# Expert weights of a hybrid decoder trunk: from the 36th matrix of a layer on, two matrices per transfer into neighbouring buffers

## The chip, the core and the metric

One Trainium2 chip, one NeuronCore of it. The metric is the device time of one execution in microseconds (us), as the median of several runs. All numbers are float32.

## What is computed

Two decoder layers on 256 tokens of 1024 features. Each layer is a mixer (one input projection, three groups of attention-like heads, one output projection) and then a mixture of 32 experts, of which each token uses 2 from one group of 8. The change touches the loading of the expert weights only. The part of the reference that reads them:

```python
D_MODEL = 1024; SEQ = 256; DEPTH = 2
N_EXPERTS = 32; TOP_K = 2; D_EXPERT = D_MODEL // 4      # 256

def hierarchical_moe(h, router_group, router_expert, router_bias, expert_gate, expert_up, expert_down):
    tok = h.reshape(b * t, d)
    ...                      # combine[n, e]: weight of expert e for token n, 2 of 32 are not zero
    for e in range(N_EXPERTS):
        y = (jax.nn.silu(tok @ expert_gate[e]) * (tok @ expert_up[e])) @ expert_down[e]
        out = out + combine[:, e:e + 1] * y.astype(jnp.float32)

for l in range(DEPTH):
    x = x + mixer(rms_norm(x, norm_mix[l]))
    x = x + hierarchical_moe(rms_norm(x, norm_ffn[l]), ...)
x = rms_norm(x, norm_final)
```

## The kernel before, in words

**Matrices and buffers.** The weights of a layer's experts are 96 MiB. On the host they are cut into 96 blocks of 1 MiB, called matrices here and numbered 0 to 95 in each layer (so the 36th is number 35). A block is 128 partitions by 2048 numbers, that is 8 KB per partition. Eight sets of four experts (QUADS) take 12 matrices each (QSLOTS): four of gate weights, four of up, four of down. Gate and up matrices hold a piece of all four experts, so every one of the first eight has to be there before the set's hidden layer is finished. SBUF has room for 25 such blocks: a ring of 12 that the mixer's weights use too, two of more_buf (N0, N1), and eleven more that the mixer gives back when it no longer needs them (C and D, S0 to S3, K and K2, L, Y, X). expert_slots (L120) lists them in the order in which they are filled, and the list is gone through again and again.

**The order of loads.** load_plan (L125) works out on the host, for each load, which buffer it fills and which use of that buffer must be over. SyncE issues nearly all transfers from one queue, in program order. For expert matrix m (L535 to L554) it waits until the buffer's last reader is counted, then issues one DMA of 1 MiB and goes on:

```python
                    b, need, _ = loads[l][NMIX + m]
                    if need:
                        sync.wait_ge(freed[need[0]], need[1])
                    src = (e_gate, e_up, e_down)[m % 12 // 4]
                    sync.dma_start(slot[b], src[l, 4 * (m // 12) + m % 4]).then_inc(arrived[b], 16)
```

The loads of the next layer's mixer weights (L515) stand behind matrix 95 in the same queue; behind the second layer's stands the final gain (L556).

**The work on them.** TensorE takes the sets in order (L1068). How many rounds a set needs depends on the routing: 32 tokens per expert fit in one, and a set of which an expert has more is gone through twice with the same weights. A round is: eight matrices of gate and up, 16 matmuls each (L1089), each preceded by a wait for the matrix (slot_of, L1072); the gather of the next round's tokens, 32 matmuls (L1058); two transposes (L1103); four down matrices, 8 matmuls each (L1110), with the sums back to the tokens between them (L1118 in the first layer, L1122 in the second), four of them between matrix 10 and matrix 11 of the set. The matmuls of L1089, L1058 and L1110 are in the program once and run in a loop; the counts here are the trace's, in which each matmul of the program stands as two. GpSimd (L587 to L589) counts a matrix as freed when TensorE is done with it in the set's last round. After the last set of layer 0 comes the second layer's mixer (L669 on), after that of layer 1 the final norm (L1424 to L1438).

Of the kernel before, what the change touches and what calls it, by code (L numbers as in the profile page):

```python
# [30 lines left out]
P = 128  # L31
LAYERS = 2
D = 1024
T = 256
# [11 lines left out]
RING = 12  # L46
WARM = 10
SLOT = 2048
# [35 lines left out]
NMIX = NPROJ + D // COLS  # L84
NMOE = 3 * EXPERTS
# [33 lines left out]

def expert_slots(ring):  # L120

    return ["N0", "N1"] + ring[0:8] + ["C", "D", "S0", "S1", "K2", "S3", "S2", "K"] + ring[8:10] + ["L"] + ring[10:12] + ["Y", "X"]


def load_plan():  # L125


    ring, last, count, landed, plan = list(range(RING)), {}, {"mix": 0, "moe": 0}, {}, []

    def gone(b, of, turns):  # L130
        count[of] += 1
        last[b] = (of, count[of])
        turns.setdefault(b, []).append(last[b])

    for _ in range(LAYERS):
        wide = expert_slots(ring)
        turns = {b: [last.get(b)] for b in ring + wide[0:2]}
        for i in range(NPROJ):
            gone(ring[i % RING], "mix", turns)
        for b in wide[10:]:  # L140
            gone(b, "mix", turns)
        mixed = count["mix"]
        for m in range(NMOE):
            gone(wide[m % len(wide)], "moe", turns)
        loads = []
        for b in [ring[i % RING] for i in range(NMIX)] + [wide[m % len(wide)] for m in range(NMOE)]:
            landed[b] = landed.get(b, 0) + 16
            loads.append((b, turns[b].pop(0), landed[b]))
        plan.append((loads, wide[NMOE % len(wide)], last["D"][1], last["Y"][1], mixed))
        ring = sorted(ring, key=lambda b: last[b][1])  # L150
    return [p[0] for p in plan], plan[-1][1], last, [p[2] for p in plan], [p[3] for p in plan], [p[4] for p in plan]

# [26 lines left out]

def trunk(nc, x_in, consts, level_masks, params, w_mix, router_w, e_gate, e_up, e_down, gain_final, row_store, out):  # L180
    loads, gain_slot, last_use, scratch_free, y_free, last_mix = load_plan()
    bank_of, uses, per_layer = {}, [0] * 8, {}
# [4 lines left out]
    with ExitStack() as ctx:  # L187
        def sb(name, shape, dt=F32):
            return ctx.enter_context(nc.sbuf_tensor(name, shape, dt))
# [41 lines left out]
        slot["K2"] = work[:, 1536 + SLOT:1536 + 2 * SLOT]  # L231
        shapes = sb("shapes", [P, NKEPT + SLOT])
        slot["C"] = shapes[:, NKEPT:NKEPT + SLOT]
        slot["D"] = sb("scratch", [P, SLOT])[:, :]
        part, o = {}, 0
# [241 lines left out]
        QSLOTS = 12  # L477
# [5 lines left out]
        def _(sync):  # L483
# [14 lines left out]
            for l in range(LAYERS):  # L498
# [3 lines left out]
                for i in range(1 - l, NMIX):  # L502
# [25 lines left out]
                    if l and i == 5:  # L528
# [5 lines left out]
                        sync.dma_start(lvl_raw, level_masks).then_inc(lvl_in, 16)  # L534
                for m in range(NMOE):  # L535
                    if m == 2:
# [7 lines left out]
                    if m == 7:  # L544
                        sync.wait_ge(mix_ready, upto(l, mix_ready, GP))
                        for h in range(MH):
                            r = 32 * (h // 2) + 4 + h % 2
                            sync.dma_start(mem[h // 2][64 * (h % 2):64 * (h % 2) + 64, :],
                                           row_store[l, 1, r:r + 1, :].to_broadcast([64, T])).then_inc(floors_in, 16)
                    b, need, _ = loads[l][NMIX + m]  # L550
                    if need:
                        sync.wait_ge(freed[need[0]], need[1])
                    src = (e_gate, e_up, e_down)[m % 12 // 4]
                    sync.dma_start(slot[b], src[l, 4 * (m // 12) + m % 4]).then_inc(arrived[b], 16)  # L554
            sync.wait_ge(moe_freed, last_use[gain_slot][1])
# [40 lines left out]
        def _(pe):  # L596
# [53 lines left out]
            for l in range(LAYERS):  # L650
# [417 lines left out]
                for q in range(QUADS):  # L1068
# [3 lines left out]
                    def slot_of(m):  # L1072

                        b, _, landed = loads[l][NMIX + QSLOTS * q + m]
                        pe.wait_ge(arrived[b], landed)
                        return slot[b]
# [919 lines left out]
```

## Time and profile before

| | us |
|---|---|
| median of 3 runs | 810.07 |
| lowest and highest | 808.99, 810.78 |
| the profiled execution, its own time | 808.36 |
| its span (first to last instruction) | 806.6 |
| TensorE busy | 770.0 (95%) |
| VectorE busy | 311.9 (39%) |
| ScalarE busy | 206.2 (26%) |

The profile is of one execution. "PE" is TensorE's matmuls, "PEld" its weight loads, which overlap them, "DVE" VectorE, "ACT" ScalarE, "SPq" the instruction stream of SyncE. A row of a timeline gives the start, the length, the engine, the line in the kernel, what was written and read, how many instructions are merged, and in brackets the idle time before them with what ended it. The granted clock (PEclk) is 1.00 at 2.4 GHz and 0.50 at 1.2 GHz. All times inside the profile count from the start of the span.

The span in words: a mixer to about 213 us, the first layer's experts to 404, a mixer to 613, the second layer's experts to 801, the final norm.

### The profile page before, as it was taken

The numbers are of one execution on the slowest core, as the hardware profiler recorded it, in microseconds if no ns is written. First come the engines' busy times: TensorE is split into PE (matmuls) and PEld (weight loads), VectorE is DVE, ScalarE is ACT, GpSimd is POOL, SyncE is SP. The second block draws the span as 40 slices with busy tenths as digits, with TensorE's granted clock in tenths as the row PEclk, the third lists the DMA queues.
The fourth block names the chain that finished last, engine by engine and source line by source line (L and its number), as shares of the span: only waits on it lengthen the run. The fifth ranks groups of instructions, "written<-read, shape, count | busy, mean of one in ns | idle before, by whom it ended". The sixth has DMA issues, their size and how long they took to land.

```text
span 806.6 us, 16492 instructions
## 1 busy us (share of the span) xinstructions
PE 770.0 (95%) x6468; PEld 548.2 (68%) x6468; DVE 311.9 (39%) x747; ACT 206.2 (26%) x436; POOL 2.9 (0%) x11
## 2 busy tenths in 40 slices
PE   8999999999999998799999999999999999999966
PEld 7877888878755554466588778888787555555523
DVE  4767343762711111111268654346635111111102
ACT  2444541531400000000124554327212000010003
POOL 0000000000000000000000000000000000000000
PEclk9999999999999999999999999999999999999998
DMA  9983264598599999999998522556977999999995
GB/s 349 418 254 101 84 234 163 158 365 358 205 423 419 419 422 418 420 422 419 420 414 287 166 105 72 222 191 237 365 304 295 422 421 420 422 419 421 420 420 227
DMA packets 44329, 256.59 MB, mean 318 GB/s; under 512 B 5024, under 2 KB 12512, under 8 KB 15456
## 3 DMA queue, kind: packets, MB, share of 16 engines
q1 hardware_dynamic: 43680, 254.77, 79.8%
q8 instruction: 49, 0.80, 0.4%
q10 hardware_dynamic: 576, 0.81, 0.3%
q14 instruction: 24, 0.20, 0.1%
HBM read 252.88 MB, written 1.64 MB: 316 GB/s over the span
## 4 chain that ended last, share of the span: by engine, by line
PE 68%; DVE 13%; DMA 13%; issue 3%; ACT 2%; SPq 1%; DVEq 0%; ACTq 0%; POOLq 0%
PE ps L1089 13%; PE ps L640 10%; PE ps L1058 8%; PE ps L1110 7%; PE ps L958 6%; PE ps L1122 4%; DMA space<-e_up 4%; DMA ring<-e_down 3%; DMA late_buf<-e_down 3%; PE ps L1118 3%; DVE xn L1474 3%; PE ps L792 3%; PE ps L849 2%; PE ps L818 2%; PE ps L669 2%
## 5 line engine op out<-in xcount | busy, mean ns | idle before, releaser
L640 PE MATMUL ps<-hT,ring 128*128 128x256 f32 x800 | 183.4, 383 | 0.1
L640 PEld LDWEIGHTS ps<-hT,ring 128*128 128x128 f32 x800 | 148.8, 190 | 22.9 <-issue 3.2
L1058 PEld LDWEIGHTS ps<-hT,xn 128*128 128x128 f32 x640 | 74.0, 194 | 9.9 <-issue 7.8
L1058 PE MATMUL ps<-hT,xn 128*128 128x128 f32 x640 | 77.8, 281 | 1.9 <-DVE hT L1821 1.9
L1089 PE MATMUL ps<-space,hT 128*32 128x256 f32 x992 | 62.9, 396 | 11.0 <-DMA space<-e_up 7.8
L958 PE MATMUL ps<-xn,ring 128*128 128x256 f32 x256 | 57.8, 382 | 0.0
L1110 PE MATMUL ps<-ring,space 128*32 128x512 f32 x416 | 51.0, 598 | 7.0 <-ACT space L1415 6.6
L1089 PEld LDWEIGHTS ps<-space,hT 128*32 128x32 f32 x992 | 30.7, 113 | 38.4 <-DMA space<-e_up 12.0
L1821 DVE TENSOR_TENSOR hT<-shapes,sel 128x128 f32<-128x128 f32 x40 | 9.9, 288 | 112.1 <-PE ps L1096 111.9
L958 PEld LDWEIGHTS ps<-xn,ring 128*128 128x128 f32 x256 | 48.2, 190 | 7.1 <-issue 0.7
L1890 DVE COPY hT<-ps 128x512 f32<-128x512 f32 x18 | 12.4, 691 | 89.1 <-PE ps L1110 89.1
L1838 DVE TENSOR_TENSOR hT<-ps,gffn 128x512 f32<-128x512 f32 x40 | 27.6, 691 | 49.7 <-PE ps L1058 49.7
L1411 ACT ACTIVATE hT<-ps 128x256 f32<-128x256 f32 x18 | 6.9, 383 | 154.4 <-PE ps L1089 154.4
L1089 PE MATMUL ps<-ring,hT 128*32 128x256 f32 x752 | 44.7, 380 | 0.0
L1415 ACT ACTIVATE space<-ps 128x256 f32<-128x256 f32 x18 | 6.9, 383 | 142.3 <-PE ps L1103 142.3
L1118 PEld LDWEIGHTS ps<-space,hT 128*128 128x128 f32 x144 | 25.2, 190 | 18.7 <-ACT hT L1417 7.5
L1118 PE MATMUL ps<-space,hT 128*128 128x256 f32 x144 | 36.1, 394 | 0.0
L1122 PE MATMUL ps<-hT,space 128*128 128x512 f32 x72 | 35.9, 622 | 0.0
L1089 PEld LDWEIGHTS ps<-ring,hT 128*32 128x32 f32 x752 | 23.5, 110 | 17.5 <-issue 3.2
L1110 PEld LDWEIGHTS ps<-ring,space 128*32 128x32 f32 x416 | 11.0, 109 | 32.1 <-issue 20.5
L1122 PEld LDWEIGHTS ps<-hT,space 128*128 128x128 f32 x72 | 11.5, 188 | 24.7 <-issue 11.8
L1887 DVE TENSOR_TENSOR hT<-hT,ps 128x256 f32<-128x256 f32 x18 | 7.6, 421 | 53.0 <-PE ps L1089 53.0
(291 smaller groups left out, 907.7 us busy)
## 6 DMA issues: line engine op xcount, KB each, us to landing
ring<-e_down SPq DMA_DIRECT2D x46, 1024.0 KB, 26.7
ring<-e_up SPq DMA_DIRECT2D x36, 1024.0 KB, 14.6
ring<-w_mix SPq DMA_DIRECT2D x33, 1024.0 KB, 9.9
space<-e_up SPq DMA_DIRECT2D x26, 1024.0 KB, 25.8
space<-e_gate SPq DMA_DIRECT2D x24, 1024.0 KB, 18.3
more_buf<-e_gate SPq DMA_DIRECT2D x14, 1024.0 KB, 10.1
ring<-e_gate SPq DMA_DIRECT2D x10, 1024.0 KB, 9.5
late_buf<-e_down SPq DMA_DIRECT2D x8, 1024.0 KB, 25.1
```

The source lines that it names most:

```text
L640: mm = pe.matmul(bank, slot_w(i)[:, k, ct * P:(ct + 1) * P], hT3[:, k, :], start=(k == 0), stop=(k == KD - 1))
L669: mm = pe.matmul(bank[:, ct * T:(ct + 1) * T], slot_w(0)[:, k, ct * P:(ct + 1) * P], hU[:, k, :], start=(k == 0 and ct == 0), stop=(k == K ...
L792: mm = pe.matmul(bank[:, j * n:(j + 1) * n], hT3[:, k, j * P:(j + 1) * P], w[:, k, 0:n], start=(k == 0), stop=(k == KD - 1))
L818: mm = pe.matmul(bank[:, j * T:(j + 1) * T], hT3[:, 4 * behind + k, j * P:(j + 1) * P], w[:, k, :], start=(behind == 0 and k == 0), stop=( ...
L958: mm = pe.matmul(ps[:, b, i * T:(i + 1) * T], w[:, i * P:(i + 1) * P], mixT[:, k, :], start=(k == 0 and i == 0), stop=(k == KD - 1 and i = ...
L1058: mm = pe.matmul(ps[:, 4 + 3 * half_, kk * P:(kk + 1) * P], xn3[:, j, k * P:(k + 1) * P], Psel[:, j, :], start=(j == 0), stop=(j == TT - 1))
L1089: mm = pe.matmul(ps[32 * e:32 * e + 32, 5 + m, 0:DE], hq[:, k, 32 * e:32 * e + 32], w[:, c0:c0 + DE], start=(k == 0), stop=(k == KD - 1), ...
L1110: mm = pe.matmul(ps[32 * e:32 * e + 32, 5 + h, :], hmT[:, f, 32 * e:32 * e + 32], w[:, e * 512:(e + 1) * 512], start=(f == 0), stop=(f == ...
L1118: mm = pe.matmul(ps[:, k // 2, k % 2 * T:(k % 2 + 1) * T], ysb[:, h, k % 4 * P:(k % 4 + 1) * P], PwT[:, 0:T], start=False, stop=False, ski ...
L1122: mm = pe.matmul(ps[:, 2 * j + h, :], PwT[:, j * P:(j + 1) * P], ysb[:, h, :], start=False, stop=False, skip_group_check=True)
L1474: link(dve.scalar_tensor_tensor(out=a, in0=s[:, t:t + T], scalar=w(t), in1=a, op0=ALU.mult, op1=ALU.add))
L1838: TTn(hq[:, half * 4:half * 4 + 4, :], ps[:, 4 + 3 * half, :].rearrange("p (k s) -> p k s", k=4), gq[:, half * 4:half * 4 + 4].unsqueeze(2 ...
```

## The change

Matrices 0 to 34 of a layer still come one by one. From matrix 35 on the list of buffers is cut into units: of 14 units, eleven are two neighbouring buffers (128 partitions by 4096 numbers, 16 KB per partition, 2 MiB) and three (L, Y and X) are single. A unit of two is one DMA with one count of arrival; TensorE waits for that same count before either matrix, and the DMA is issued when both buffers are free. For this D moves behind C into the tensor shapes, S3 and S2 change places in the order, and K comes before K2. On the host the three weight arrays become one, experts_w, in which each unit lies in the order of its transfer, so that a partition's 16 KB of two matrices are contiguous. Matrix 95 is a unit by itself, since the layer ends in the middle of the list. The mixer's loads, the matmuls and their order stay.

```diff
--- before.py
+++ after.py
@@ -117,9 +117,19 @@
 COPIES = 3
 
-def expert_slots(ring):
-
-    return ["N0", "N1"] + ring[0:8] + ["C", "D", "S0", "S1", "K2", "S3", "S2", "K"] + ring[8:10] + ["L"] + ring[10:12] + ["Y", "X"]
+def expert_loads(ring):
+
+    pairs = [ring[i:i + 2] for i in range(0, RING, 2)]
+    assert all(i % 2 == 0 and j == i + 1 for i, j in pairs)
+    return ([["N0", "N1"]] + pairs[0:4] + [["C", "D"], ["S0", "S1"], ["S2", "S3"], ["K", "K2"], pairs[4], ["L"], pairs[5], ["Y"], ["X"]])
+
+
+LEAD = 5
+
+
+def mixer_gives(ring):
+
+    return ["C", "D", "S0", "S1", "K2", "S3", "S2", "K"] + ring[8:10] + ["L"] + ring[10:12] + ["Y", "X"]
 
 def load_plan():
@@ -133,22 +143,41 @@
         turns.setdefault(b, []).append(last[b])
     for _ in range(LAYERS):
-        wide = expert_slots(ring)
-        turns = {b: [last.get(b)] for b in ring + wide[0:2]}
+        ahead = [[b] for b in ["N0", "N1"] + ring[0:8] + mixer_gives(ring)]
+        cycle = expert_loads(ring)
+        units = ahead + [[b] for bufs in cycle[0:LEAD] for b in bufs] + cycle[LEAD:]
+        while sum(len(bufs) for bufs in units) <= NMOE:
+            units += cycle
+        order = [b for bufs in units for b in bufs]
+        turns = {b: [last.get(b)] for b in ring + order[0:2]}
         for i in range(NPROJ):
             gone(ring[i % RING], "mix", turns)
-        for b in wide[10:]:
+        for b in mixer_gives(ring):
             gone(b, "mix", turns)
         mixed = count["mix"]
         for m in range(NMOE):
-            gone(wide[m % len(wide)], "moe", turns)
+            gone(order[m], "moe", turns)
         loads = []
-        for b in [ring[i % RING] for i in range(NMIX)] + [wide[m % len(wide)] for m in range(NMOE)]:
+        for b in [ring[i % RING] for i in range(NMIX)]:
             landed[b] = landed.get(b, 0) + 16
             loads.append((b, turns[b].pop(0), landed[b]))
-        plan.append((loads, wide[NMOE % len(wide)], last["D"][1], last["Y"][1], mixed))
+        parts, place, m = [], [], 0
+        for bufs in units:
+            bufs = bufs[0:NMOE - m]
+            if not bufs:
+                break
+            landed[bufs[0]] = landed.get(bufs[0], 0) + 16
+            needs = {}
+            for b in bufs:
+                need = turns[b].pop(0)
+                if need:
+                    needs[need[0]] = max(need[1], needs.get(need[0], 0))
+            parts.append((m, bufs, needs, landed[bufs[0]]))
+            place += [(b, bufs[0], landed[bufs[0]]) for b in bufs]
+            m += len(bufs)
+        plan.append((loads, order[NMOE], last["D"][1], last["Y"][1], mixed, parts, place))
         ring = sorted(ring, key=lambda b: last[b][1])
-    return [p[0] for p in plan], plan[-1][1], last, [p[2] for p in plan], [p[3] for p in plan], [p[4] for p in plan]
+    return [p[0] for p in plan], plan[-1][1], last, [p[2] for p in plan], [p[3] for p in plan], [p[4] for p in plan], [p[5] for p in plan], [p[6] for p in plan]
 
 def psum_plan():
...
@@ -229,9 +258,15 @@
         slot["Y"] = space[:, 0:SLOT]
         slot["K"] = work[:, 1536:1536 + SLOT]
         slot["K2"] = work[:, 1536 + SLOT:1536 + 2 * SLOT]
-        shapes = sb("shapes", [P, NKEPT + SLOT])
+        shapes = sb("shapes", [P, NKEPT + 2 * SLOT])
         slot["C"] = shapes[:, NKEPT:NKEPT + SLOT]
-        slot["D"] = sb("scratch", [P, SLOT])[:, :]
+        slot["D"] = shapes[:, NKEPT + SLOT:NKEPT + 2 * SLOT]
+        slot_pair = {i: ring[:, i:i + 2, :].rearrange("p a c -> p (a c)") for i in range(0, RING, 2)}
+        slot_pair["N0"] = more_buf[:, :, :].rearrange("p a c -> p (a c)")
+        slot_pair["C"] = shapes[:, NKEPT:NKEPT + 2 * SLOT]
+        for i in (0, 2):
+            slot_pair[f"S{i}"] = shared[:, T + i * SLOT:T + (i + 2) * SLOT]
+        slot_pair["K"] = work[:, 1536:1536 + 2 * SLOT]
...
@@ -532,7 +567,7 @@
...
-                for m in range(NMOE):
+                for m, bufs, needs, _ in expert_units[l]:
                     if m == 2:
                         swap_halves(1)
                     if m == 6:
@@ -547,11 +582,11 @@
                             r = 32 * (h // 2) + 4 + h % 2
                             sync.dma_start(mem[h // 2][64 * (h % 2):64 * (h % 2) + 64, :],
                                            row_store[l, 1, r:r + 1, :].to_broadcast([64, T])).then_inc(floors_in, 16)
-                    b, need, _ = loads[l][NMIX + m]
-                    if need:
-                        sync.wait_ge(freed[need[0]], need[1])
-                    src = (e_gate, e_up, e_down)[m % 12 // 4]
-                    sync.dma_start(slot[b], src[l, 4 * (m // 12) + m % 4]).then_inc(arrived[b], 16)
+                    for of, n in needs.items():
+                        sync.wait_ge(freed[of], n)
+                    n = len(bufs)
+                    src = experts_w[l, m * P * SLOT:(m + n) * P * SLOT].rearrange("(p c) -> p c", p=P)
+                    sync.dma_start(slot[bufs[0]] if n == 1 else slot_pair[bufs[0]], src).then_inc(arrived[bufs[0]], 16)
...
@@ -1071,8 +1106,8 @@
                     def slot_of(m):
-                        b, _, landed = loads[l][NMIX + QSLOTS * q + m]
-                        pe.wait_ge(arrived[b], landed)
+                        b, lead, landed = expert_place[l][QSLOTS * q + m]
+                        pe.wait_ge(arrived[lead], landed)
...
@@ -1977,13 +2012,16 @@
     down = features_by_tile(g["expert_down"]).reshape(LAYERS, QUADS, 4, P, 2, 2, 512).transpose(0, 1, 5, 4, 3, 2, 6)
     experts = [rows_by_slot(g["expert_gate"]), rows_by_slot(g["expert_up"]), down.reshape(LAYERS, EXPERTS, P, SLOT)]
+    units = load_plan()[6]
+    experts_w = np.stack([np.concatenate([np.stack([experts[m % 12 // 4][l, 4 * (m // 12) + m % 4] for m in range(m0, m0 + len(bufs))], 1).reshape(-1)
+                                          for m0, bufs, _, _ in units[l]]) for l in range(LAYERS)])
...
```

What moves in the queue of SyncE, at the two places that matter below. The names in a row are the tensor written and the array read (more_buf holds N0 and N1, shapes holds C, space holds S0 to S3, K, K2 and Y, xT is X, late_buf is L); x4 is four DMAs in a row.

SyncE, first layer, before: the matrices 60 (shapes) to 72 (the last row here), that is the sixth set and the first matrix of the seventh.

```order
L554 DMA shapes<-e_gate 128x2048
L554 DMA scratch<-e_gate 128x2048
L554 DMA space<-e_gate 128x2048 x2
L554 DMA space<-e_up 128x2048 x4
L554 DMA ring<-e_down 128x2048 x2
L554 DMA late_buf<-e_down 128x2048
L554 DMA ring<-e_down 128x2048
L554 DMA ring<-e_gate 128x2048
```

The same 13 matrices in the changed kernel: 60 and 61; 62 and 63, 64 and 65, 66 and 67; 68 and 69; 70; 71 and 72.

```order
L589 DMA shapes<-experts_w 128x4096
L589 DMA space<-experts_w 128x4096 x3
L589 DMA ring<-experts_w 128x4096
L589 DMA late_buf<-experts_w 128x2048
L589 DMA ring<-experts_w 128x4096
```

Thirteen DMAs have become seven, and matrix 71, the last of the sixth set, now shares a transfer with matrix 72, the first of the seventh.

SyncE, second layer, before: the last matrices, 84 (the ring's first row here) to 95, and the load behind them.

```order
L554 DMA ring<-e_gate 128x2048
L554 DMA shapes<-e_gate 128x2048
L554 DMA scratch<-e_gate 128x2048
L554 DMA space<-e_gate 128x2048
L554 DMA space<-e_up 128x2048 x4
L554 DMA space<-e_down 128x2048
L554 DMA ring<-e_down 128x2048 x2
L554 DMA late_buf<-e_down 128x2048
L556 DMA ring<-gain_final 128x1024
```

The changed kernel from matrix 77 to 95: four units of the ring (77 to 84), 85 and 86, then 87 and 88, 89 and 90, 91 and 92 in space, 93 and 94, and 95.

```order
L589 DMA ring<-experts_w 128x4096 x4
L589 DMA shapes<-experts_w 128x4096
L589 DMA space<-experts_w 128x4096 x3
L589 DMA ring<-experts_w 128x4096
L589 DMA late_buf<-experts_w 128x2048
L591 DMA ring<-gain_final 128x1024
```

Matrix 91, the last of the up weights, now shares a transfer with matrix 92, the first of the down weights. The end of the first layer's experts has the same units.

## Rows read from the trace of the kernel before

**Rows 1.** The page, part 2: the span in 40 equal slices.

```profile
PE   8999999999999998799999999999999999999966
DMA  9983264598599999999998522556977999999995
GB/s 349 418 254 101 84 234 163 158 365 358 205 423 419 419 422 418 420 422 419 420 414 287 166 105 72 222 191 237 365 304 295 422 421 420 422 419 421 420 420 227
```

**Rows 2.** The timeline, TensorE: first layer, first round of matrices 60 to 71.

```profile
318.14 1.07 PE L1089 MATMUL ps<-space,hT 128*32 128x256 f32 x16 [0.64 <-DMA space<-e_gate]
...
330.44 1.07 PE L1089 MATMUL ps<-space,hT 128*32 128x256 f32 x16 [0.92 <-DMA space<-e_up]
331.44 3.84 PE L1058 MATMUL ps<-hT,xn 128*128 128x128 f32 x32
...
338.87 1.13 PE L1118 MATMUL ps<-space,hT 128*128 128x256 f32 x4
340.36 1.07 PE L1110 MATMUL ps<-ring,space 128*32 128x512 f32 x8 [0.36 <-DMA ring<-e_down]
```

**Rows 3.** The timeline, TensorE: last round of the first layer.

```profile
391.09 3.84 PE L1058 MATMUL ps<-hT,xn 128*128 128x128 f32 x32
...
398.48 1.13 PE L1118 MATMUL ps<-space,hT 128*128 128x256 f32 x4
...
399.97 1.07 PE L1110 MATMUL ps<-late_buf,space 128*32 128x512 f32 x8 [0.36 <-DMA late_buf<-e_down]
```

**Rows 4.** The timeline, TensorE: last round of the second layer.

```profile
773.71 1.07 PE L1089 MATMUL ps<-scratch,hT 128*32 128x256 f32 x16 [1.44 <-DMA scratch<-e_gate]
...
786.02 1.62 PE L1089 MATMUL ps<-space,hT 128*32 128x256 f32 x16 [1.42 <-DMA space<-e_up]
787.57 4.89 PE L1058 MATMUL ps<-hT,xn 128*128 128x128 f32 x32
...
795.89 1.13 PE L1122 MATMUL ps<-hT,space 128*128 128x512 f32 x2
...
796.94 1.06 PE L1110 MATMUL ps<-late_buf,space 128*32 128x512 f32 x8
```

**Rows 5.** Waits of SyncE's queue from 236 to 404 us: total, times, longest.

```profile
SPq L554 <- POOLq L589: 65.0, 35, 6.6
```

**Rows 6.** Line 554 from 236 to 404 us: issue to landing of its transfers.

```profile
DMA to landing us min/median/max: 16.3/27.0/31.4
```

**Rows 7.** The timeline, TensorE: both rounds of matrices 36 to 47, second layer.

```profile
672.04 1.07 PE L1089 MATMUL ps<-scratch,hT 128*32 128x256 f32 x16
...
691.70 1.07 PE L1089 MATMUL ps<-scratch,hT 128*32 128x256 f32 x16
```

**Rows 8.** Windows: busy time of PE, PEld, DVE, ACT, POOL, then PEclk, DMA share, GB/s.

```profile
228.00:232.00 4.00, 3.53 (x32) 1.32 (x30) 0.69 (x1) 0.98 (x2) 0.00 (x0) 1.00 1.02 432
18.00:40.00 22.00, 22.00 (x124) 19.03 (x123) 16.40 (x46) 8.21 (x19) 0.00 (x0) 1.00 1.02 417
240.00:400.00 160.00, 149.57 (x1628) 88.83 (x1621) 27.16 (x63) 14.90 (x33) 0.00 (x0) 0.99 1.01 420
618.00:770.00 152.00, 148.22 (x1554) 78.46 (x1546) 27.32 (x62) 12.90 (x30) 0.00 (x0) 1.00 1.01 421
```

**Rows 9.** The page, part 6: the mixer's loads with 4 KB per partition.

```profile
ring<-w_mix SPq DMA_DIRECT2D x14, 512.0 KB, 15.9
```

**Rows 10.** The page, part 2: all packets by size.

```profile
DMA packets 44329, 256.59 MB, mean 318 GB/s; under 512 B 5024, under 2 KB 12512, under 8 KB 15456
```

**Rows 11.** The page, part 3: DMA queues, packets, MB, share of 16 engines.

```profile
q8 instruction: 49, 0.80, 0.4%
```

**Rows 12.** Windows around the last wait of the second layer, same columns.

```profile
786.00:790.00 4.00, 3.98 (x28) 2.93 (x29) 0.42 (x1) 0.00 (x0) 0.00 (x0) 0.57 1.02 422
780.00:786.00 6.00, 2.26 (x36) 0.84 (x32) 0.01 (x1) 0.00 (x0) 0.00 (x0) 1.00 1.01 419
```

More of the change, by code:

```diff
@@ L177, in psum_plan, with trunk @@
     return front + inv + late
-def trunk(nc, x_in, consts, level_masks, params, w_mix, router_w, e_gate, e_up, e_down, gain_final, row_store, out):
-    loads, gain_slot, last_use, scratch_free, y_free, last_mix = load_plan()
+def trunk(nc, x_in, consts, level_masks, params, w_mix, router_w, experts_w, gain_final, row_store, out):
+    loads, gain_slot, last_use, scratch_free, y_free, last_mix, expert_units, expert_place = load_plan()
     bank_of, uses, per_layer = {}, [0] * 8, {}
@@ L1985 @@
     for name, a in [("x_in", x_in), ("consts", consts), ("level_masks", level_masks), ("params", params), ("w_mix", w_mix),
-                    ("router_w", router_w), ("e_gate", experts[0]), ("e_up", experts[1]), ("e_down", experts[2]),
+                    ("router_w", router_w), ("experts_w", experts_w),
                     ("gain_final", gain_final)]:
```

## The prediction

> **What bounds the kernel now.** I began with the page's 40 slices [rows 1], to see where TensorE and where the transfers are the limit. TensorE is at 9 tenths nearly everywhere. The DMA engines are at 9 tenths from 222 to 423 us and from 625 to 787 us, at 414 to 423 GB/s: in the experts' stages 96 MiB per layer have to come in, and the two limits lie close together. To tell which one ends last I read TensorE's timeline for waits that a transfer ends. It has them at three places only.
>
> First, in the first layer, round one of matrices 60 to 71 (this set is gone through twice): TensorE has caught up with the stream and waits for nearly every matrix, and last for matrix 71, at 340.36 [rows 2]. Second, the first layer's last matrix, 95, at 399.97 [rows 3]. Third, the second layer's last set, from matrix 86 at 773.71 to matrix 91 at 786.02 [rows 4]; after 91 comes no wait for a transfer any more, not even for 95. Everything else on the way to the end is TensorE's or VectorE's own work.
>
> At all three places the stream had been running without a gap. SyncE waited for a freed buffer 35 times, 65 us in all [rows 5], and yet the transfers landed 16 to 31 us after their issue [rows 6]: there was always a queue ahead of them. So an earlier issue gains nothing, and a later one costs nothing up to some 13 us (the 16 less the transfer's own 2.5). From 340.36 (matrix 71) to 399.97 (matrix 95) 24 matrices landed, 2.48 us each [rows 2, 3]. That is the step of everything below.
>
> **The change, part by part.**
>
> *Fewer DMAs to issue* (27 fewer per layer), other waits in front of them, and other places in SBUF: nothing. A pair is issued when its second buffer is free, mostly one matrix later than its first would have been, 0.9 to 6 us of TensorE's time, under the 13 us. The longest case is the pair 60 and 61 in the second layer: it waits for the buffer of matrix 36, whose set is gone through twice, from 672.04 and again from 691.70 [rows 7], so it goes out at about 692.6 and not at 672. Matrix 59 lands near 786.0 - 32 x 2.48 = 706.6; 14 us are left. If that queue were not there, the pairs would cost just what they are issued later. The first 35 matrices, where the queue builds up, stay single. TensorE waits on a count that has been reached as often as before.
>
> *Later landing of a pair's first matrix.* A count that stands for 2 MiB is reached when the second matrix is in, 2.48 us later. Of the three places two depend on it. Matrix 71 now comes with 72, so the round that ended on it ends 2.48 us later: the round's up matrices (66 and 67 together at the time of 67) are done 0.9 us later than now, in time for that. Matrix 91 now comes with 92: again 2.48 us. Matrix 95 is single; its wait held TensorE for 0.43 us (1.49 us from the start before it to its own [rows 3], against 1.05 without a wait, 795.89 to 796.94 [rows 4]), and since TensorE then arrives later, that wait goes. Sum: 2.48 - 0.43 + 2.48 = **+4.5 us**, if the stream keeps its rate.
>
> The other pairs at these places cost nothing: 62 to 67 and 85 to 90 are waited for in twos, but the last of them arrives as before.
>
> *The rate of the stream.* The trace of before has no row of 16 KB, so this is bounded. I compare rows of 8 KB with rows of 4 KB. From 240 to 400 and from 618 to 770 only 8 KB rows move: 420 and 421 GB/s. From 18 to 40 us mixer loads move, at 417 [rows 8]; five of them are of the kind with 4 KB rows [rows 9], 2.6 of 9.2 MB. For that mean the 4 KB rows have to move at about 408 GB/s. On one of 16 engines that is 160.4 ns for a 4 KB row and 311.7 ns for an 8 KB row; so a row costs some 9 ns beside its bytes (6 to 12 with the rounding of the rates). A matrix is 8 rows per engine. Two matrices as 8 rows of 16 KB instead of 16 of 8 KB save 8 x 9 = 73 ns, **0.036 us per matrix** (0.026 to 0.048), which makes about 427 GB/s. The bounds: 0 if a row's cost stays what it is, or a little under, since nothing excludes that longer rows fit the memory worse (I take -0.01); and 0.07, if the stream went at 432 GB/s, the best 4 us of the trace [rows 8]. I take 0.036, for it comes from the rows nearest to the question. It lifts no wait by itself; it makes the stream run ahead, and what is late next is the work of TensorE.
>
> That 4 KB and 8 KB rows are each one packet fits the packet counts [rows 10], and the instruction queue's 49 packets for 0.80 MB [rows 11] show that a packet of 16 KB exists. Neither proves it for this queue.
>
> How often it counts: until matrix 72 has landed, 34 matrices of the layer came in pairs (35 to 72 without 45, 48, 49 and 70): 34 x 0.036 = 1.24 us. Until 92 in the second layer it is 52 (without 73 and 74 too): 1.89 us. In the first layer the pair 91 and 92 is not on the path: 92 would land at about 392.4 - 1.9 = 390.5, and TensorE, 1.2 us late from matrix 71 on, needs 91 at 391.
>
> **The sum.** First layer: 2.48 - 1.24 - 0.43 = +0.8 us. It moves the second layer as a whole, its stream too, since that starts with buffers that TensorE frees. Second layer: 2.48 - 1.89 = +0.6 us. Together **+1.4 us**; in general 4.5 - 86 x the saving per matrix. Against the profiled execution's 808.36 us that is 809.8; that execution lies 1.7 us under the median of 810.07, and the change goes on the median: **811.5 us**. A measurement of this kernel can tell about 0.2% (1.6 us) from no change, so the forecast is "no change, on its slow side".
>
> A rule speaks against any gain in rate. The Trainium skill (DMA: Bandwidth & Descriptors, Bandwidth) says that for transfers from HBM the limit is HBM's share of a core, about 358 GB/s; by that, row length would be without effect and the sum +4.5. The trace disagrees on the number: 420 [rows 8] on a core that runs alone. It is rival A with its own evidence below.
>
> **The rivals.**
>
> *A, slower: the rows get no cheaper* (the change does not do what it says: a 16 KB row is moved as two of 8 KB, or the 9 ns are not a row's cost but something else of the first 40 us). Then only the later landings remain: +4.5 us, 814.6. For it: the 417 against 420 is a small difference, in a stretch where other small transfers run too. Against: the 4 KB rows are the only large thing that differs there. It decides from a saving under 0.034 per matrix on, where the sum passes 1.6 us. That is close to my own figure. Chance 0.17.
>
> *B, faster: the stream reaches the best rate seen.* 0.07 per matrix: 4.5 - 6.0 = -1.5 us, 0.3 of it in the first layer and 1.2 in the second: 808.6. Beyond that the first layer ends on TensorE's own work, which gives no more than its 0.43. For it: the 432 GB/s [rows 8]. Against: that is over 4 us, where the landing of one transfer counts 6%. Chance 0.10. The Trainium skill (the same page, Where 436 GB/s comes from) puts the ceiling at 435 GB/s and says to batch into large transfers. An estimate from that page's ceiling: 0.07 per matrix again, so the same time.
>
> *C, slower: the clock.* After the wait for 91 TensorE ran at its lower level, 1.2 GHz, for part of 786 to 790 (mean 0.57 [rows 12]), after 6 us in which it was busy for 2.26. The gather then took 4.89 us and the matrix's matmuls 1.62 against 3.84 and 1.07 elsewhere [rows 2, 3]: 1.6 us already in the time of before. With pairs the waits are fewer but longer, some 3 us with 1.8 us of work between them. If the lower level lasts through the gather, up to as much again is lost: +1.6 on top, 813.1. In the first layer the same slowing would be covered by the wait for 71. It could as well fall before the landing and give back up to 1.6. Chance 0.13.
>
> **How the numbers follow.** My own case has 0.60. Its range is +0.4 to +2.3 from the saving per matrix, and about 1.6 wider below and 0.1 above for the clock: 809 to 812.5. Over all cases 808.8 to 815.0: this leaves out most of B, the lower edge of my case and what lies above A. Slower by over 0.2%: all of A, 0.10 of C, 0.21 of my case: 0.48. Faster: 0.08 of B and 0.04 of mine: 0.12. The rest, 0.40, is within 0.2%.
>
> **What the profile of the changed kernel would show.** The rate in the full stretches 426 to 428 GB/s (420 for A, 432 for B), and packets fewer by some 6900 (54 pairs x 128) if a 16 KB row is one packet, equal if not. Waits of TensorE for transfers in twos, about 3 us long, in round one of 60 to 71, the last of them at about 341.6 instead of 340.36. No wait for matrix 95 of the first layer. The second mixer beginning 0.8 us later. In the last round the wait for 91 ending near 787.4. I would be wrong if a wait for a transfer stood at a fourth place, above all early in a stage (the queue had run dry), or if the mixers' lengths changed.

## The result, and the profile after

The changed kernel takes 811.13 us (median of 22 runs, 808.92 to 813.16) against 809.60 us (22 runs, 808.02 to 810.78) of the kernel before beside it: ratio 1.002, 95% interval 1.0014 to 1.0027. By the ratio that is 1.6 us or 0.2% more, and the whole interval lies above 1. The forecast was 1.4 us more, in a range of -1.3 to +4.9. Changes in us of other kernels below are worked out from their ratios in the same way.

The profiled execution took 812.13 us, with a span of 810.3; it is one of the slower of its 22, 3.8 us above the profiled one of before. So the profile shows more than the medians do, and the part that is too much has to be found in it. The page, part 2:

```profile
PEclk9999999999999999899999999999999999999998
DMA  9982264498599999999996532656977999999994
GB/s 348 418 250 96 88 234 162 156 364 358 211 421 428 423 428 427 423 430 424 420 416 208 174 105 66 221 195 220 366 316 288 425 425 424 429 429 424 427 425 173
DMA packets 36553, 256.58 MB, mean 317 GB/s; under 512 B 4160, under 2 KB 11648, under 8 KB 14592
```

Against [rows 1] the full stretches went up from 414 to 423 to 416 to 430 GB/s. Against [rows 10] there are 7776 packets fewer: 54 pairs x 128 rows of 16 KB that had been two rows of 8 KB, and 54 x 16 small ones (under 512 B: 5024 to 4160). So a row of 16 KB is one packet. Windows of the three stretches of [rows 8] (the second layer's from 620 us), columns as there:

```profile
18.00:40.00 22.00, 22.00 (x124) 19.07 (x124) 16.32 (x46) 8.20 (x19) 0.00 (x0) 1.00 1.02 418
240.00:400.00 160.00, 147.78 (x1616) 89.47 (x1609) 27.18 (x63) 13.02 (x31) 0.00 (x0) 0.98 1.01 425
620.00:770.00 150.00, 146.15 (x1558) 78.00 (x1554) 27.19 (x63) 13.62 (x32) 0.00 (x0) 1.00 1.01 426
```

SyncE's waits and its transfers' landing times, 236 to 404 us (line 589 is before's 554):

```profile
SPq L589 <- POOLq L624: 93.1, 30, 16.1
```

```profile
DMA to landing us min/median/max: 17.9/35.8/47.6
```

SyncE waits longer for freed buffers than in [rows 5], and yet the transfers land 18 to 48 us after their issue, not 16 to 31 [rows 6]: there is more in front of them than before. In this stretch a late issue costs nothing.

TensorE's timeline, first layer. Line 1124 is before's 1089, 1093 is 1058, 1145 is 1110, 1153 is 1118:

```profile
320.59 1.94 PE L1124 MATMUL ps<-space,hT 128*32 128x256 f32 x32 [2.49 <-DMA space<-experts_w]
...
325.25 3.32 PE L1124 MATMUL ps<-space,hT 128*32 128x256 f32 x32 [2.36 <-DMA space<-experts_w]
...
330.15 1.93 PE L1124 MATMUL ps<-space,hT 128*32 128x256 f32 x32 [1.58 <-DMA space<-experts_w]
332.01 3.84 PE L1093 MATMUL ps<-hT,xn 128*128 128x128 f32 x32
...
339.27 1.13 PE L1153 MATMUL ps<-space,hT 128*128 128x256 f32 x4
342.41 1.70 PE L1145 MATMUL ps<-ring,space 128*32 128x512 f32 x8 [2.01 <-DMA ring<-experts_w]
344.04 3.87 PE L1153 MATMUL ps<-space,hT 128*128 128x256 f32 x12
...
402.00 1.13 PE L1153 MATMUL ps<-space,hT 128*128 128x256 f32 x4
403.06 1.07 PE L1145 MATMUL ps<-late_buf,space 128*32 128x512 f32 x8
```

Up to 330 us these are the waits of [rows 2], now in twos. Then the wait for matrix 71, which has grown from 0.36 to 2.01 us and ends at 342.41, not at 340.36. And a thing that I had put elsewhere: behind that wait the matmuls of 71 take 1.70 us and the sums after them 3.87, against 1.06 and 2.88 at full clock. The window 342 to 348 of this profile, and of the kernel of e3 below, which is the same up to there:

```profile
342.00:348.00 6.00, 5.59 (x24) 3.27 (x28) 0.69 (x1) 0.00 (x0) 0.00 (x0) 0.72 1.03 434
```

```profile
342.00:348.00 6.00, 4.87 (x40) 2.94 (x44) 0.69 (x1) 0.00 (x0) 0.00 (x0) 1.00 1.02 429
```

The granted clock averaged 0.72 here and 1.00 there: 1.6 us (0.64 + 0.99), in this execution. Matrix 95 is not waited for any more.

The second layer, from the first gather (612.60; before 609.29) on:

```profile
612.60 3.84 PE L1093 MATMUL ps<-hT,xn 128*128 128x128 f32 x32 [0.93 <-DVE hT L1856]
...
770.19 1.06 PE L1145 MATMUL ps<-ring,space 128*32 128x512 f32 x8 [0.26 <-DMA ring<-experts_w]
...
780.00 1.94 PE L1124 MATMUL ps<-space,hT 128*32 128x256 f32 x16 [2.97 <-DMA space<-experts_w]
...
784.87 1.93 PE L1124 MATMUL ps<-space,hT 128*32 128x256 f32 x32 [1.08 <-DMA space<-experts_w]
789.76 1.91 PE L1124 MATMUL ps<-space,hT 128*32 128x256 f32 x16 [2.96 <-DMA space<-experts_w]
791.60 4.62 PE L1093 MATMUL ps<-hT,xn 128*128 128x128 f32 x32
...
800.70 1.07 PE L1145 MATMUL ps<-late_buf,space 128*32 128x512 f32 x8
```

The wait for 91 still ends the stream's part, now with 92 and after 2.96 us of idleness. Two pairs landed one after the other, 4.89 us apart (784.87, 789.76); two single matrices took 4.97 (781.05 to 786.02, the first from the same timeline of before as [rows 4]).

To compare kernels whose executions begin their experts at slightly different times (213.4 to 214.9 us in all twelve profiles), I measure each layer's experts from the start of their first gather. "71" and "91" are the starts of those matrices' matmuls in the first and in the second layer, "95" the start of the last matrix's, "gather" the length of the one behind 91. In e2 and e3 only one of the two pairs is apart; the other kernels are described below. Every row is one execution, and what one execution loses to the lower clock is in it.

| kernel | ratio to before | 1st layer: 71 | 1st: 95 | 2nd: 91 | gather | 2nd: 95 |
|---|---|---|---|---|---|---|
| before | 1 | 126.92 | 186.53 | 176.73 | 4.89 | 187.65 |
| the change | 1.002 | 128.38 | 189.03 | 177.16 | 4.62 | 188.10 |
| e1 both apart | 0.9958 | 126.57 | 185.60 | 174.76 | 3.84 | 185.05 |
| e2 71 apart | 1.0003 | 128.13 | 187.16 | 177.25 | 3.84 | 186.56 |
| e3 91 apart | 0.9973 | 128.44 | 187.46 | 174.93 | 3.84 | 185.23 |
| e4 two DMAs | 1.0045 | 129.57 | 188.63 | 179.06 | 5.28 | 189.97 |
| e7 both apart, pairs from 25 on | 0.9975 | 127.25 | 186.29 | 175.78 | 3.84 | 186.07 |
| e8 three apart | 0.9966 | 127.99 | 187.03 | 174.71 | 3.84 | 184.62 |
| e9 all apart | 0.9993 | 128.00 | 187.02 | 176.62 | 3.84 | 186.78 |
| e11 as e1 | 0.9968 | 127.91 | 186.93 | 174.72 | 3.84 | 185.01 |

Between 95 and the next layer's first gather lie 209.32 us in before and 209.54 with the change: the mixers kept their length.

### The profile page after: what moved, and what is told of

It is laid out like the page before. It is cut to its first block, busy times and chain, and to the rows that moved or that the text cites. A ratio compares the mean times of both kernels' runs of the same rounds, so it can differ in the third digit from the quotient of the medians.

```text
span 810.3 us, 16438 instructions
## 1 busy us (share of the span) xinstructions
PE 771.4 (95%) x6468; PEld 548.6 (68%) x6468; DVE 312.4 (39%) x747; ACT 206.1 (25%) x436; POOL 2.9 (0%) x11
## 2 busy tenths in 40 slices
DMA packets 36553, 256.58 MB, mean 317 GB/s; under 512 B 4160, under 2 KB 11648, under 8 KB 14592
## 4 chain that ended last, share of the span: by engine, by line
PE 67%; DMA 14%; DVE 13%; issue 3%; ACT 2%; DVEq 0%; SPq 0%; ACTq 0%; POOLq 0%
PE ps L1124 13%; PE ps L675 10%; PE ps L1093 8%; PE ps L1145 7%; PE ps L993 6%; DMA space<-experts_w 6%; DMA ring<-experts_w 6%; PE ps L1153 4%; PE ps L1157 3%; DVE xn L1509 3%; PE ps L827 3%; PE ps L884 2%; PE ps L853 2%; PE ps L704 2%; PE ps L917 1%
```

## The experiments

My theory (landing): a pair costs only where its first matrix is waited for on the path, at 71 and at 91, 2.48 us each, and the longer rows give some 0.036 us per matrix back. Rivals: the pairs are issued too late (issue); the lower clock makes the loss (clock); the longer rows give nothing.

**e1: the two pairs taken apart, in both layers.**

```diff
+SPLIT = (71, 91)
...
+        whole, m0 = [], 0
+        for bufs in units:
+            whole += [[b] for b in bufs] if m0 in SPLIT else [bufs]
+            m0 += len(bufs)
+        units = whole
         order = [b for bufs in units for b in bufs]
```

> The changed kernel with the units (71, 72) and (91, 92) taken apart into single loads, in both layers; 25 pairs per layer stay. Landing theory (the pairs cost only where the first of them is waited for and the wait is on the path, that is at 71 and at 91, and the rows of 16 KB save 0.03 to 0.036 us per matrix everywhere): both waits end 2.48 us earlier than with the change, the first layer ends 0.9 us earlier than before (on TensorE's own work), the second gains 1.5 to 1.8 us more: 2.4 to 2.7 us faster than before, ratio 0.9967 to 0.9970. Issue theory (what the change loses comes from pairs being issued late): taking two of 27 pairs apart changes next to nothing, ratio 1.001 to 1.002. Clock theory (the loss is mostly the lower clock after longer waits): faster than with the change by about the 1.6 us of matrix 71, not more, ratio about 1.000.

Measured: 805.97 us, ratio 0.9958 (0.9945 to 0.9970), 3.4 us less than before and about 5 less than the change (by the ratios). Its timeline around both places (line 1159 is before's 1118, 1151 is 1110, 1099 is 1058, 1130 is 1089):

```profile
330.55 1.93 PE L1130 MATMUL ps<-space,hT 128*32 128x256 f32 x32 [1.36 <-DMA space<-experts_w]
...
339.68 1.13 PE L1159 MATMUL ps<-space,hT 128*128 128x256 f32 x4
340.74 1.06 PE L1151 MATMUL ps<-ring,space 128*32 128x512 f32 x8
...
399.77 1.07 PE L1151 MATMUL ps<-late_buf,space 128*32 128x512 f32 x8
...
609.12 3.84 PE L1099 MATMUL ps<-hT,xn 128*128 128x128 f32 x32 [0.93 <-DVE hT L1862]
...
783.88 1.07 PE L1130 MATMUL ps<-space,hT 128*32 128x256 f32 x16 [0.55 <-DMA space<-experts_w]
784.88 3.84 PE L1099 MATMUL ps<-hT,xn 128*128 128x128 f32 x32
...
791.26 1.92 PE L1151 MATMUL ps<-ring,space 128*32 128x512 f32 x16 [0.76 <-DMA ring<-experts_w]
...
794.17 1.06 PE L1151 MATMUL ps<-late_buf,space 128*32 128x512 f32 x8
```

Matrix 71 is there when TensorE comes (0.35 us earlier than before), and 91 starts 1.97 us earlier than before in its layer: 48 paired matrices before it by 0.036 would be 1.73. The issue theory is out, for 25 pairs are left and nothing of the loss. So is the clock as the main cause, for which the ratio would be about 1.000. Taking a pair apart also issues its first matrix earlier, but that is not the reason: in the profile of the change every transfer of line 589 issued from 296 to 404 us landed 26.8 us or more after its issue, every one from 700 to 790 at least 22.0 us after, and from 300 to 348 us the DMA engines' share stayed at 0.99 or above (means of 3 to 10 us). The landing theory holds, and the time falls a little below its range. The rows show why: behind a wait of 0.55 us the gather runs at full clock, 3.84 us and not 4.89. A new wait of 0.76 us, for the pair 93 and 94, takes some of that back. The first layer is 0.93 us shorter than before in this profile; no other with 71 apart gained more than 0.24 there (see e8).

**e2 and e3: one of the two taken apart.** The edit is that of e1 with SPLIT = (71,) or (91,).

> Only (71, 72) taken apart. Landing theory: the first layer ends 0.9 us earlier than before and not 0.8 (or, with the lower clock behind the wait, up to 3) later; the second layer loses the 0.6 us that the change loses there: ratio about 0.9996, and the wait for matrix 71 in the trace is 0 to 0.4 us long. Issue theory: as with the change, 1.001 to 1.002.

> Only (91, 92) taken apart. Landing theory: the first layer as with the change, 0.8 to 1.5 us later than before; the second layer gains 1.5 to 1.8 us against before: ratio 0.9990 to 1.0000. In the trace the wait for 91 ends about 2.4 us earlier against the start of the second layer's experts than with the change. Issue theory: 1.001 to 1.002.

Measured: e2 1.0003 (0.9994 to 1.0012), e3 0.9973 (0.9962 to 0.9983). e2 lies on its forecast within the interval, though not by the way foreseen alone: a slow gather in round one (4.91 us) made TensorE late for 71, so that this layer is 0.6 us longer than before and not 0.9 shorter. The second layer is 1.1 us shorter, though 91 and 92 still share a transfer: here the lower clock fell in front of the landing (3.25 us for the matmuls of 89 and 90, against 1.93), and behind it the matmuls of 91 took 1.07 and the gather 3.84. e3 is 1.4 us or more faster than expected. At 91 itself it is as forecast (174.93 against 176.73, 1.8 us). Behind it the matmuls and the gather run at full clock, 1.07 and 3.84 us against 1.62 and 4.89, which gives 1.6 us, and a wait of 0.78 us for 93 takes about half of it back. That makes 1.5 us for the two layers of this profile; what is left to the measured 2.2 is not shown. These are its rows:

```profile
343.13 1.06 PE L1151 MATMUL ps<-ring,space 128*32 128x512 f32 x8 [2.00 <-DMA ring<-experts_w]
344.13 2.88 PE L1159 MATMUL ps<-space,hT 128*128 128x256 f32 x12
...
786.42 1.07 PE L1130 MATMUL ps<-space,hT 128*32 128x256 f32 x16 [0.55 <-DMA space<-experts_w]
787.42 3.84 PE L1099 MATMUL ps<-hT,xn 128*128 128x128 f32 x32
```

The first two are the control for the clock: the same wait for 71 as with the change (2.00 us), and behind it full speed. So the plan with its wait does not settle it; one execution loses the 1.6 us and another does not. (e5 below, with a wait of 2.17 us at this place, lost 1.5: 1.93 us for the matmuls of 71 and 3.52 for the sums.)

**e4: the units as they are, loaded by two DMAs each.** This is the later landing without the longer rows.

```diff
-            landed[bufs[0]] = landed.get(bufs[0], 0) + 16
+            landed[bufs[0]] = landed.get(bufs[0], 0) + 16 * len(bufs)
...
-                    sync.dma_start(slot[bufs[0]] if n == 1 else slot_pair[bufs[0]], src).then_inc(arrived[bufs[0]], 16)
+                    for i, b in enumerate(bufs):
+                        sync.dma_start(slot[b], src[:, i * SLOT:(i + 1) * SLOT]).then_inc(arrived[bufs[0]], 16)
```

> The units, their waits and their common count of arrival stay, but each unit is loaded by two DMAs of 1 MiB with rows of 8 KB (out of the same array, rows 16 KB apart): the later landing without the longer rows. Landing theory: the stream goes at 420 GB/s again and the whole of 4.5 us shows, ratio 1.0050 to 1.0056. If the longer rows gave nothing, it equals the change, 1.002.

Measured: 813.73 us, 1.0045 (1.0032 to 1.0058). Its windows:

```profile
240.00:400.00 160.00, 148.21 (x1624) 89.34 (x1620) 27.17 (x63) 13.01 (x31) 0.00 (x0) 0.98 1.01 420
620.00:770.00 150.00, 145.10 (x1552) 77.53 (x1552) 27.17 (x63) 13.62 (x32) 0.00 (x0) 1.00 1.01 421
```

The rate is that of before, and 71 and 91 start 2.65 and 2.33 us later than before in their layers, both behind a wait for the transfer (0.56 and 3.03 us): the 2.48 twice. The time is a little under the forecast, which is inside its interval. So the longer rows are worth 0.25% (1.0045 to 1.002), and without them the change would cost twice as much and more.

**e5 and e6: one DMA of 2 MiB, with rows of 8 KB and of 4 KB.** The host lays a unit out in two blocks of 128 rows in e5 and in four in e6. This is e5's load of a pair; e6 has 4 for the 2, and the host's part is left out:

```diff
+                        sync.dma_start(slot_pair[bufs[0]].rearrange("p (a c) -> p a c", a=2),
+                                       src.rearrange("(a p c) -> p a c", a=2, p=P)).then_inc(arrived[bufs[0]], 16)
```

> The changed kernel, each unit of two still one DMA of 2 MiB, but laid out in memory as two blocks, so that it moves as 256 rows of 8 KB and not 128 of 16 KB. If the saving belongs to the row (my 9 ns per row), the full stretches fall back from 425 to 426 GB/s to 420 to 421 and the time is that of two DMAs per unit, ratio 1.004 to 1.006. If it belongs to the DMA (fewer counts of arrival, fewer issues), the rate stays 425 to 426 and the ratio 1.002.

> The same with rows of 4 KB, four blocks of 128 rows per half... 512 rows per unit in one DMA. At 9 ns per row the units go at 408 to 409 GB/s: the first layer ends 4 us later than before (now on the stream, at its last matrix), the second loses 6.5 to 7 us more: ratio 1.013 to 1.015. If a row costs nothing: 1.002 to 1.005.

Measured: e5 1.0050 (1.0035 to 1.0064), e6 1.0129 (1.0114 to 1.0145). e5's packets and first window, then e6's:

```profile
DMA packets 43465, 256.58 MB, mean 316 GB/s; under 512 B 4160, under 2 KB 11648, under 8 KB 14592
240.00:400.00 160.00, 147.30 (x1608) 89.12 (x1600) 26.83 (x63) 12.75 (x31) 0.00 (x0) 0.98 1.01 420
```

```profile
DMA packets 57289, 256.58 MB, mean 313 GB/s; under 512 B 4160, under 2 KB 11648, under 8 KB 42240
240.00:400.00 160.00, 145.63 (x1588) 87.08 (x1581) 25.80 (x61) 12.69 (x30) 0.00 (x0) 0.98 1.02 410
```

e5 has the small packets of the change (4160, so as few DMAs) and the rows of before, and it has the rate of before. The saving belongs to the row, not to the DMA. Rows of 4, 8 and 16 KB give 410, 420 and 425 to 426 GB/s. Per matrix that is 2.56, 2.49 (at 420.5) and 2.46 us. With some 54 of 64 matrices of the stretch in pairs, a paired matrix of e6 takes 0.076 us more (8 rows per engine more) and one of the change 0.035 us less (4 rows fewer). As an estimate that is 9.5 and 8.7 ns per row, to about 1 and 2 ns, since the view gives whole GB/s. e6's time is just under the lower edge of its forecast, e5's in the middle.

**e8: the pair 93 and 94 taken apart as well.** The edit is that of e1 with SPLIT = (71, 91, 93).

> As the kernel without the pairs (71, 72) and (91, 92), with (93, 94) taken apart too: in that one TensorE waited 0.76 us for 93 in the second layer. Landing theory: that wait goes, ratio 0.9945 to 0.9955. If the wait only moves on to matrix 95, as before, 0.9958.

Measured: 0.9966 (0.9954 to 0.9979), a miss. The wait for 93 is gone and one of 0.31 us for 95 is there. The second layer's experts were the shortest of all (184.62 us to matrix 95, against 185.05 in e1), but the first layer's took 187.03 in this profile against 185.60. Up to matrix 92 that first layer has the same plan as e1's. The rows show what differs:

```profile
329.87 3.52 PE L1130 MATMUL ps<-space,hT 128*32 128x256 f32 x32 [2.51 <-DMA space<-experts_w]
333.32 3.84 PE L1099 MATMUL ps<-hT,xn 128*128 128x128 f32 x32
...
341.63 1.07 PE L1151 MATMUL ps<-ring,space 128*32 128x512 f32 x8
```

The matmuls of 66 and 67 took 3.52 us and not the 1.93 of e1. From their start to the start of 71 TensorE needed 10.19 us in e1 and 11.8 in e2, e7, e8 and e11, in these four at the lower clock for a part (in e2, e7 and e11 that part reached into the gather). With 71 apart nothing covers these 1.6 us; with the pair (71, 72) the wait for it does, which ends 12.26 us after the same start with the change and in e3. So at 71 the pair costs 1.8 us against e1, but only 0.4 to 0.5 against e8 and e11. e1's profile has the one good first layer of four with pairs from 35 on and 71 apart, and is the fastest of its five executions. The gain of 0.4 us that was expected of e8 is smaller than this, and with their intervals e1 and e8 are not to be told apart.

**e9: every unit taken apart.** What is left is one array and the moved buffers: the edit of e1 without its condition.

> The changed kernel with every unit taken apart: one array, the buffers at their new places (D in shapes, the order S2 S3 K K2), no pair. What is left of the change beside the pairs: 0.9995 to 1.0005 if that is nothing, as predicted. The mixers began the first experts 0.6 to 1.2 us later in all five profiles of kernels with pairs; if the new places did that, 1.0007 to 1.0015.

Measured: 0.9993 (0.9984 to 1.0002). The rest of the change makes no difference that can be measured. Its profile began the experts latest of all, at 214.9 us, but the time of its 11 runs leaves out the 1.0007 to 1.0015 that the new places would have cost. Its first layer, which has no pair, also shows the lower clock in front of 71 (4.80 us for the gather of round one, against 3.84 before), so that this is no matter of pairs. In this profile the granted clock was 0.89 from 9 to 20 us, against 1.00 before, which goes with the late start; e3 and e7 began nearly as late at full clock there, and why stays open.

**e7 and e11: pairs from matrix 25 on, and e1 once more beside it.** Both have e1's edit with SPLIT = (71, 91); e7 has this one as well:

```diff
-LEAD = 5
+LEAD = 0
```

> As the kernel without the pairs (71, 72) and (91, 92), and pairs from matrix 25 on (LEAD 0) instead of 35. Landing theory with a queue that never runs dry: the first layer as there (it ends on TensorE's work), the second gains 10 x 0.034 = 0.3 us more: 0.3 us faster than that kernel, ratio about 0.9955. Issue theory: here, at the start of the experts, the queue is still short, a pair goes out only when its second buffer is free, and the DMA engines stand idle for up to 0.9 us per layer; then it is 0.5 to 1 us slower than that kernel, and the windows from 214 to 226 us show less than there.

> The kernel without the pairs (71, 72) and (91, 92) once more, beside the one with LEAD 0 on the same chip: ratio 0.9950 to 0.9966 again.

Measured: e7 0.9975 (0.9966 to 0.9984), e11 0.9968 (0.9957 to 0.9979). The difference is inside the intervals, but the profiles tell the two apart. Windows where the first layer's experts begin, e7 first, then e11:

```profile
218.00:222.00 4.00, 4.00 (x69) 2.27 (x68) 2.10 (x8) 0.60 (x2) 0.00 (x0) 1.00 0.95 305
222.00:226.00 4.00, 4.00 (x67) 2.22 (x67) 1.03 (x5) 0.72 (x2) 0.00 (x0) 1.00 0.85 352
```

```profile
218.00:222.00 4.00, 4.00 (x70) 2.27 (x68) 2.18 (x9) 0.72 (x1) 0.00 (x0) 1.00 0.91 336
222.00:226.00 4.00, 4.00 (x71) 2.22 (x67) 0.99 (x4) 0.72 (x2) 0.00 (x0) 1.00 1.01 420
```

With pairs from 25 on the DMA engines move 305 and 352 GB/s where they moved 336 and 420. In the second layer it is the same, e7 first, then e11:

```profile
614.00:618.00 4.00, 4.00 (x70) 2.22 (x73) 2.10 (x8) 0.38 (x2) 0.00 (x0) 1.00 0.85 268
618.00:622.00 4.00, 4.00 (x69) 2.39 (x64) 1.40 (x5) 0.34 (x2) 0.00 (x0) 1.00 0.91 383
```

```profile
614.00:618.00 4.00, 4.00 (x71) 2.51 (x69) 2.41 (x10) 0.00 (x0) 0.00 (x0) 1.00 0.93 336
618.00:622.00 4.00, 4.00 (x74) 2.18 (x66) 0.99 (x4) 0.72 (x2) 0.00 (x0) 1.00 1.00 418
```

By 622 us e7 has moved 0.08 MB less in this layer, although its experts began 0.76 us earlier: together it is 0.9 us behind. Its second layer reaches matrix 91 after 175.78 us instead of 174.72 and matrix 95 after 186.07 instead of 185.01. I had expected 0.3 us of gain and got 1.1 us of loss there. Here the issue theory is right: at the start nothing waits in the queue, and a pair that goes out when its second buffer is free leaves a gap. In its first layer e7 lost nothing by it (186.29 us against 186.93), for that layer ends on TensorE's own work. Loading matrices 25 to 34 singly is worth about 1 us of the second layer in these profiles; the medians don't show it.

## Why the prediction was right

**The bound and the three places.** Right. With the change the stream ran at its full rate to the end of both layers, TensorE's waits stood at the first layer's round one and at the second layer's end, and the wait for 95 in the first layer was gone. One thing was overlooked: a fourth, in the second layer for matrix 83, 0.26 us at 770.19, since 83 now comes with 84. The prediction had named a wait at a fourth place as the sign that it was wrong. This one is not early in the stage and costs nothing, for TensorE waits for the stream behind it anyway (2.97 us at 780.00); the sign was drawn too wide.

**The later landing, 2.48 us at 71 and at 91.** Right, and shown from both sides: e4 has 2.65 and 2.33 us with the rate kept; e1 is without them. At 91 the profiles agree closely: 177.16 and 177.25 us with the pair (the change, e2), 174.71 to 174.93 without (e1, e3, e8, e11). At 71 what the pair costs depends on when TensorE arrives, 0.4 to 1.8 us.

**The rate, 0.036 us per matrix and 427 GB/s.** Right in size (425 to 426 with the single loads among them, 0.035), and the extrapolation from rows of 4 and 8 KB is borne out by e5 and e6: the cost goes by the row. Rival A, that a 16 KB row is moved as two, is out by the packets. So is rival B: over 150 us and more the stream went at 425 to 426, not at 432. The limit of about 358 GB/s that the Trainium skill gives (DMA: Bandwidth & Descriptors, Bandwidth) does not bind this core: 420 before and 425 after. The same section gives that figure as a core's share when both cores of a pair stream; the prediction had it as a limit of any core. Rival B's estimate from the Trainium skill's ceiling of 435 GB/s (the same page, Where 436 GB/s comes from) comes to 0.08 us per matrix at the 420.5 of [rows 8], not 0.07; nothing hangs on it.

**The sum.** Forecast +1.24 us at 71 and, in the second layer, +0.59 at 91. Measured +1.46 and +0.43. With the 0.43 us of matrix 95 gone, the first layer should have been 0.8 us longer; it is 0.93 in e3, which has the same plan there but for 91, which the first layer does not wait for, and 2.50 in the profile of the change. The difference is the clock. The times that the prediction named came later: 71 at 342.41 and not near 341.6, the end of the wait for 91 at 789.76 and not near 787.4. Of both 0.59 us are the later start of the experts in this execution, and of the second 1.6 us are the clock at 71. That the forecast and the medians agree to 0.2 us is partly luck. The terms of the sum were right in kind and nearly in size, but each layer of one execution is 1.6 us longer or shorter by where the clock falls (the second layer of e2 has the change's plan but for 71, reaches 91 within 0.1 us of it, and is 1.5 us shorter at 95). The forecast's range had room for that, its middle had not.

**The clock (rival C).** The mechanism was right, its place only in part. I had looked for it behind 91 and held the first layer to be covered by the wait for 71. But the 2 us at 71 are themselves a wait that the clock can fall behind. There the profiled execution lost 1.6 us; with a wait of 2.00 us e3 lost nothing. Behind 91 the matmuls and the gather took 1.91 and 4.62 us with the change and 1.62 and 4.89 before, so nothing was added. Rival C's other half was right too: in e2 the lower clock fell in front of the landing of 91 and 92, and the 1.6 us behind it were not lost. That this is also what spreads the 22 runs over 4.2 us (2.8 before) is likely, and was not shown: a run has only its mean clock.

**Nothing for the rest.** Right for the moved buffers and the single array (e9), and for the fewer DMAs (e5 against e4, 1.0050 and 1.0045, inside their intervals). That a pair may be issued later for free holds from matrix 35 on and not from 25 on (e7).

## What to carry to other kernels

Where loads are coalesced, look at which pieces share a transfer: a pair costs a full piece of waiting if its first member ends a stage on the path and its second belongs to the next. Here two such pairs of 27 turned a gain of 0.3 to 0.4% (e1, e11) into a loss of 0.2%. Coalesce where a queue stands in front of the transfers, and load singly where the queue is still empty and where the stage's last piece is waited for; e1, which does so, beats both kernels. And don't read a term of 1 us out of one profile against another before you have looked where the lower clock fell in each.

## What the runs showed of the hardware

In the full stretches the stream ran at 410 GB/s where most rows were of 4 KB (e6), at 420 to 421 with 8 KB (before, e4, e5) and at 425 to 426 with 16 KB (the change). As an estimate from these rates a row costs about 9 ns on its DMA engine beside its bytes, whether 8 KB rows come in DMAs of 1 MiB or of 2 MiB. A 16 KB row was one packet, and each DMA of an expert matrix or pair had 16 packets under 512 B of its own; saving 54 x 16 of them moved neither rate nor time measurably (e5 against e4). TensorE's clock after a wait of 2 to 3 us is not settled by the plan: behind the wait for 71 it was 0.50 for a part in two executions (the change, e5), 1.5 to 1.6 us dearer, and 1.00 throughout in a third (e3).
